# A mixture-of-experts layer: adding the expert outputs to the residual by selection matmuls instead of through DRAM

## Chip, cores, metric

One core of one Trainium2 chip. The metric is the device time of one launch in microseconds; the kernel before took 1423.31 us (median of 3 runs, 1421.72 to 1424.41).

## What is computed

One encoder layer on 512 tokens of width 1024 in f32: four parallel token mixers and their merge, attention over 256 memory tokens, and a mixture of experts; then a last RMSNorm. The mixture sends each token to 2 of 32 experts:

```
h = rmsnorm(x);  group = argmax(h @ w_group + b_group);  two experts = top 2 of softmax(router logits of the group)
for each expert e, on its tokens:  y = (silu(h @ w1[e]) * (h @ w3[e])) @ w2[e]      # 1024 -> 512 -> 1024
x = x + sum over the token's two experts of weight * y;   out = rmsnorm(x) * final_norm
```

## The kernel before

The mixers and the attention fill the first 828 us and are not touched. The mixture has two stages.

**Routing** (L1500 to L1690). The rows after the norm go to DRAM (`xn_scratch`). DVE finds each token's experts and its two weights (`wsel`). `pos` is the token's place in each expert's list, `cnt` an expert's number of tokens. From them come `idx` (the first 64 tokens of each expert, one column an expert) and `idy` (the rows of `ys_scratch` to which the outputs go); a full list of tokens for each expert is written to DRAM by eight scatters of 128 elements (L1855). DVE also makes a table of jobs: one row of four integers for each further block of 64 tokens of an expert that has over 64. With these inputs there is one such overflow job.

**Experts** (from L1695). `experts(lo, hi)` runs on each engine over the 32 experts q, with the job between expert 15 and 16 (`MID` = 16).
- SP loads the weights: six pieces of 1 MB an expert, in order, into a ring of 18 buffers (three experts deep, `DEEP`). A piece is issued when TensorE has used up the one that lies in its buffer (`consumed`, L1744). The job's six pieces take a turn of the ring (L1811), and expert 18 waits for the end of the job (`o_xo`).
- POOL gathers 64 rows an expert from `xn_scratch` (`fetch`, L1839, two experts ahead) and scatters the output to `ys_scratch` (`store`, L1846). For the job it waits for the stores, loads the job's place (a register) and the list, waits for DVE's indices, and gathers (L1867 to L1875).
- PE turns the rows (`turn_rows`, e_x, L1754), multiplies by w1 and w3 (`up`, e_u, L1769: two column halves of 64 tokens side by side), turns the hidden rows (`turn_hidden`, e_h, L1760) and multiplies by w2 (`down`, e_y, L1779). Its order in turn q is up(q), turn_rows(q+1), turn_hidden(q-1), down(q-1).
- ACT copies the turned rows (L1969, L1974), makes tanh and a copy (L1979, L1981), and copies the output to `yo` (L1986). DVE has two products an expert (L2048, L2053).
- At the end SP loads the 4 MB of `ys_scratch` (L1825), DVE adds them to the residual `x_sb`, tile t by tile (L2086, 128 tokens each), and the last norm follows: Square and Sqrt on ACT (L2020, L2022), scaling on DVE (L2080), the store (L1828).

All waits are written out by hand; each engine takes its instructions in the order of the text.

## Time and profile before

| | us |
|---|---|
| median of 3 runs | 1423.31 |
| the profiled execution | 1424.24 |
| its span, first to last instruction | 1422.6 |
| experts, from the first gather to the last scaling | 871.65 to 1419.55 |
| mean granted TensorE clock | 0.963 |

The page gives busy times of the engines, then 40 slices of 35.6 us each: the slices from the 25th on are the experts. A row of the chain says what the end of the program was waiting for at that time; a row of a stretch says how much each engine and the 16 DMA engines were busy in it.

### The profile page before, as it was taken

What the parts mean: (1) busy time and instruction counts of PE and PEld (TensorE: products, weight loads), DVE (VectorE), ACT (ScalarE), POOL (GpSimd) and SP (SyncE); (2) the same over time, 40 slices, a digit from 0 to 9 for tenths busy, and PEclk for the clock granted to TensorE, in tenths of its full rate; (3) what the DMA queues carried; (4) which work ended last, traced back from release to release, by engine and by line L of the source; (5) the groups of instructions that cost most, each with busy time, mean ns of one, the idle gap of its engine ahead of it and who ended that gap; (6) DMA issues with size and microseconds to landing.
All of it is one profiled execution on the core that took longest, in us unless ns stands there. A gap on an engine that the chain in (4) does not pass through costs nothing. (4 is left out here: it accounts for less than half of the span.)

```text
span 1422.6 us, 15467 instructions
## 1 busy us (share of the span) xinstructions
PE 1223.8 (86%) x6254; PEld 828.3 (58%) x6254; DVE 527.9 (37%) x948; ACT 387.3 (27%) x638; POOL 92.2 (6%) x118
## 2 busy tenths in 40 slices
PE   6999999999999988999998864997777489887782
PEld 5887997897687766888886532333333133333330
DVE  4333444667857387445365434110100001010004
ACT  6222232235443432243253220121111112111112
POOL 1000000000000000000000003111111101111100
PEclk9999999999999999999999986999999789999996
DMA  7322213112123212323331069999999979999994
GB/s 266 112 88 76 75 60 115 64 60 82 45 71 107 89 67 100 137 90 107 115 113 66 0 270 322 366 409 408 416 417 407 419 310 396 406 416 415 411 401 184
DMA packets 50470, 301.54 MB, mean 212 GB/s; under 512 B 8882, under 2 KB 9282, under 8 KB 20320
## 3 DMA queue, kind: packets, MB, share of 16 engines
q1 hardware_dynamic: 41792, 281.06, 51.1%
q0 software_dynamic: 8080, 17.41, 3.7%
q10 hardware_dynamic: 528, 2.10, 0.4%
q8 instruction: 50, 0.82, 0.2%
q14 instruction: 20, 0.16, 0.0%
HBM read 296.50 MB, written 12.93 MB: 218 GB/s over the span
## 5 line engine op out<-in xcount | busy, mean ns | idle before, releaser
L1769 PE MATMUL e_u<-w_raw,xT 128*64 128x512 f32 x1056 | 244.0, 608 | 62.1 <-DMA w_raw<-in_w 58.7
L1769 PEld LDWEIGHTS e_u<-w_raw,xT 128*64 128x64 f32 x1056 | 81.6, 139 | 219.7 <-issue 215.6
L2048 DVE SCALAR_TENSOR_TENSOR tn<-tn,e_u 64x512 f32<-64x512 f32 x32 | 21.7, 679 | 429.5 <-ACT tn L1979 429.5
L286 DVE TENSOR_TENSOR s_lo<-s_raw,s_hi 128x2048 fp32r<-128x2048 f32 (+1 forms) x68 | 138.5, 2037 | 42.5 <-ACT s_hi L281 41.5
L281 ACT CAST s_hi<-s_raw 128x2048 fp32r<-128x2048 f32 (+1 forms) x68 | 115.8, 1703 | 104.6 <-PE pz L529 34.7
L1779 PE MATMUL e_y<-w_raw,hidT 128*64 128x512 f32 x528 | 121.9, 604 | 15.4 <-ACT hidT L1974 15.0
L513 PE MATMUL pz<-hT_hi,s_hi 128*128 128x512 f32 x256 | 103.7, 405 | 10.1 <-DVE s_lo L286 10.1
L497 PE MATMUL pz<-hT_hi,s_hi 128*128 128x512 f32 x256 | 102.9, 402 | 0.0
L1969 ACT COPY xT<-e_x 128x512 f32<-128x512 f32 x32 | 18.7, 585 | 306.5 <-PE e_x L1754 306.5
L513 PE MATMUL pz<-hT_hi,s_lo 128*128 128x512 f32 x256 | 101.0, 394 | 0.0
L513 PE MATMUL pz<-hT_lo,s_hi 128*128 128x512 f32 x256 | 100.9, 394 | 0.0
L497 PE MATMUL pz<-hT_lo,s_hi 128*128 128x512 f32 x256 | 99.9, 390 | 0.0
L497 PE MATMUL pz<-hT_hi,s_lo 128*128 128x512 f32 x256 | 99.8, 390 | 0.0
L1779 PEld LDWEIGHTS e_y<-w_raw,hidT 128*64 128x64 f32 x528 | 35.3, 138 | 77.6 <-issue 57.5
L490 PE MATMUL pz<-s_hi,hT_hi 128*128 128x256 f32 x256 | 73.5, 287 | 0.0
L490 PE MATMUL pz<-s_lo,hT_hi 128*128 128x256 f32 x256 | 72.4, 283 | 0.0
L490 PE MATMUL pz<-s_hi,hT_lo 128*128 128x256 f32 x256 | 72.4, 283 | 0.0
L529 PE MATMUL pz<-zR,s_hi 128*128 128x512 f32 x192 | 63.0, 389 | 0.0
L513 PEld LDWEIGHTS pz<-hT_hi,s_hi 128*128 128x128 f32 x256 | 48.7, 190 | 22.6 <-DVE s_lo L286 11.8
L1846 POOL DMA_INDIRECT ys_scratch<-yo,idy x32 | 32.0, 1001 | 390.9 <-ACT yo L1986 390.9
L920 ACT ACTIVATE tg<-pz 128x512 f32<-128x512 f32 x32 | 19.1, 598 | 134.5 <-PE pz L513 134.5
L513 PEld LDWEIGHTS pz<-hT_hi,s_lo 128*128 128x128 f32 x256 | 49.0, 191 | 10.8 <-issue 1.0
(355 smaller groups left out, 1904.9 us busy)
## 6 DMA issues: line engine op xcount, KB each, us to landing
w_raw<-in_w SPq DMA_DIRECT2D x198, 1024.0 KB, 27.3
s_raw<-in_w_mix SPq DMA_DIRECT2D x30, 1024.0 KB, 4.8
s_raw<-in_w_gb SPq DMA_DIRECT2D x32, 768.0 KB, 4.2
s_raw<-in_w_out_pieces SPq DMA_DIRECT2D x4, 1024.0 KB, 5.0
w_raw<-ys_scratch SPq DMA_DIRECT2D x8, 512.0 KB, 6.6
x_sb<-in_x SPq DMA_DIRECT2D x4, 512.0 KB, 4.7
rel_bias<-in_rel_tiles POOLq DMA_DIRECT2D x8, 256.0 KB, 3.1
decay<-in_decay POOLq DMA_DIRECT2D x8, 256.0 KB, 4.0
```

The lines of the kernel that those rows point to most:

```text
L281: nc.scalar.copy(w_hi[n % 2][:, 0:w], w_raw[n % 2][:, 0:w]).then_inc(w_himade, 1)
L286: nc.vector.tensor_tensor(w_lo[n % 2][:, 0:w], w_raw[n % 2][:, 0:w], w_hi[n % 2][:, 0:w].bitcast(F32), ALU.subtract).then_inc(w_split, 1)
L490: last = nc.tensor.matmul(pz[j][:, half * CW:(half + 1) * CW], hp[:, k, at:at + P], wp, start=(k == 0 and m == 0), stop=(k == KD - 1 and m ...
L497: last = nc.tensor.matmul(pz[j][:], wp, hp, start=(k == 0 and m == 0), stop=(k == KD - 1 and m == 2))
L513: last = nc.tensor.matmul(pz[0][:], wp, hp, start=(k == 0 and m == 0), stop=(k == KD - 1 and m == 2))
L529: last = nc.tensor.matmul(pz[1][:], wp, yp[:, k, :], start=(k == 0 and m == 0), stop=(k == KB - 1 and m == 2))
L920: nc.scalar.activation(tg[u % 2][:], pz[0][:], ACT.Tanh, scale=0.5).then_inc(g_tanh, 1)
L1769: m = nc.tensor.matmul(ps_u[o][lo:lo + FIRST, :], xT[b][:, k * FIRST:(k + 1) * FIRST], raw[j][:, kk * FF:(kk + 1) * FF], start=k == 0, sto ...
L1779: m = nc.tensor.matmul(ps_y[o][lo:lo + FIRST, :], hT[b][:, k * FIRST:(k + 1) * FIRST], raw[j][:, kk * D + h * FF:kk * D + (h + 1) * FF], s ...
L1846: pool.indirect_dma_start(ys_halves, bass.IndirectOffsetOnAxis(idy[:, q:q + 1], 0), yo[b][:], None, bounds_check=last_y, oob_is_err=False) ...
L1969: nc.scalar.copy(xT[q % 2][:], ps_x[:]).then_inc(s_xT, 1)
L2048: nc.vector.scalar_tensor_tensor(tn[:], tn[:], 1.0, ps_u[b][0:FIRST, :], ALU.add, ALU.mult).then_inc(s_hm, 1)
```

## The change

- No `ys_scratch`, no `store`, no load of 4 MB at the end, no `idy`. ACT's copy of an output gets the type float32r (`y_hi`), DVE makes the rest `y_lo` = output - `y_hi`.
- After the routing DVE makes `wq` (a token's weight for each expert) and `pos_if` (place + 1 where the token is the expert's), PE turns the latter to `pos_rows` (32 x 512).
- For each expert `select` (one matmul) spreads the expert's row of `pos_rows` over 128 partitions in the PSUM of e_x, and DVE compares it with the slot number (`selected`): `st` is 1 where slot and token meet. `unit(q, t)` multiplies `st` by `y_hi` and `y_lo` for token tile t: 4 matmuls of 64 rows, 128 columns by 512, for the two halves h of the width in the two row halves of the array and two PSUM banks. DVE adds `wq` times the result to `x_sb` (`add`, two instructions a unit). A unit waits for the adds of the one before. The units of expert q-2 stand in turn q: after each half of up, after turn_hidden, and after down(q-1); those of expert 30 stand before down(31), those of 31 at the end.
- The job's list, table row and token rows are fetched by POOL in turns 8 and 10, and DVE makes its indices and weights (`job_ids`) in turn 10. Each job fetches the next one's; there is one fetch more than jobs. The job's outputs are added by 8 matmuls and 8 adds.
- For that the job table, now 17 rows, is written by SP to DRAM a second time with each row 128 times (`job_of_all`), ahead of the loads for expert 3.

The diff, cut:

```diff
...
-        ys_dram = nc.dram_tensor("ys_scratch", [SLOTS, D], F32).ap()
         list_dram = nc.dram_tensor("list_scratch", [EXPERTS * LIST, 1], I32).ap()
         jobs_dram = nc.dram_tensor("jobs_scratch", [1, P], I32).ap()
+        job_of_all = nc.dram_tensor("jobs_wide", [JOBS + 1, P, 4], I32).ap()
...
+                wide = [P, T, EXPERTS]
+                do.after(nc.vector.tensor_tensor(junk[:, 0, :, :], hot[:, 0, :, :],
+                                                 wsel[:, 0, :].unsqueeze(2).to_broadcast(wide), ALU.mult))
+                do.after(nc.vector.tensor_tensor(junk[:, 1, :, :], hot[:, 1, :, :],
+                                                 wsel[:, 1, :].unsqueeze(2).to_broadcast(wide), ALU.mult))
+                do.after(nc.vector.tensor_tensor(wq[:], junk[:, 0, :, :], junk[:, 1, :, :], ALU.add))
...
-                do.after(nc.vector.tensor_scalar(idy[:], idf[:], 2.0, half_no, ALU.mult, ALU.add))
...
+                sp.dma_start(jobs_dram[0:1, 0:4 * (JOBS + 1)].rearrange("o (j q) -> (o j) q", q=4),
+                             jobsi[0:JOBS + 1, :]).then_inc(s_jobs_out, 16)
+                sp.dma_start(job_of_all, jobsi[0:JOBS + 1, :].unsqueeze(1).to_broadcast([JOBS + 1, P, 4])
+                             ).then_inc(s_jobs_wide, 16)
...
+                consumed(sp, END, W2A)
                 sp.dma_start(final_gain, bass.AP(a["rows"].tensor, 0, [[0, P], [1, D]])).then_inc(f_gain, 16)
-                for b in range(2):
-                    sp.wait_ge(s_ys[b], 16 * (EXPERTS // 2))
-                for t in range(T):
-                    for ch in range(2):
-                        r = ch * N + t * P
-                        sp.dma_start(y_of(t, ch), ys_dram[r:r + P, :]).then_inc(f_ld[ch][t], 16)
...
-                def store(q):
-                    b = q % 2
-                    pool.wait_ge(s_yo, q + 1)
-                    pool.indirect_dma_start(ys_halves, bass.IndirectOffsetOnAxis(idy[:, q:q + 1], 0),
-                                            yo[b][:], None,
-                                            bounds_check=last_y, oob_is_err=False).then_inc(s_ys[b], 16)
...
+                def list_of(r):
+                    j = pool.value_load(jobs_dram[0:1, bass.ds(r * 4, 1)], min_val=0,
+                                        max_val=(EXPERTS * LIST - FIRST) // LIST_UNIT)
+                    for lo in (0, FIRST):
+                        pool.dma_start(ibl[lo:lo + FIRST, :], list_dram[bass.ds(j * LIST_UNIT, FIRST), :].bitcast(U32)
+                                       ).then_inc(s_lst, 16)
+                    pool.dma_start(jb[:], job_of_all[bass.ds(r, 1), :, :].rearrange("o p q -> (o p) q")
+                                   ).then_inc(s_lst, 16)
+
+                def rows_of_job():
+                    pool.indirect_dma_start(xo[:], None, xn_dram,
+                                            bass.IndirectOffsetOnAxis(ibx[0:FIRST, :], 0),
+                                            bounds_check=last_x, oob_is_err=False).then_inc(o_xs, 16)
+
                 for q in range(MID):
                     fetch(q + 2)
-                    if q:
-                        store(q - 1)
-                store(MID - 1)
-                pool.wait_ge(s_scattered, 16 * 2 * T)
-                pool.wait_ge(s_jobs_out, 16)
+                    if q == LIST_AT:
+                        pool.wait_ge(s_scattered, 16 * 2 * T)
+                        pool.wait_ge(s_jobs_out, 16)
+                        pool.wait_ge(s_jobs_wide, 16)
+                        list_of(0)
+                    if q == LIST_AT + 2:
+                        pool.wait_ge(s_ids, 1)
+                        pool.wait_ge(o_zero, 1)
+                        rows_of_job()
...
+                        pool.wait_ge(o_cu, r * 8 + 8)
                         pool.sem_inc(s_turn, 1)
-                        pool.indirect_dma_start(xo[:], None, xn_dram,
-                                                bass.IndirectOffsetOnAxis(ibx[0:FIRST, :], 0),
-                                                bounds_check=last_x, oob_is_err=False).then_inc(o_xs, 16)
-                        pool.wait_ge(o_yo, r + 1)
+                        list_of(r + 1)
+                        pool.wait_ge(s_ids, r + 2)
                         pool.sem_inc(s_turn, 1)
-                        pool.indirect_dma_start(ys_halves, bass.IndirectOffsetOnAxis(iby[:], 0),
-                                                yoo[:], None,
-                                                bounds_check=last_y, oob_is_err=False).then_inc(o_ys, 16)
-                        pool.wait_ge(o_ys, r * 16 + 16)
+                        rows_of_job()
...
-                for q in range(MID, EXPERTS):
-                    if q + 2 < EXPERTS:
-                        fetch(q + 2)
-                    if q > MID:
-                        store(q - 1)
-                store(LAST)
-                for b in range(2):
-                    pool.wait_ge(s_ys[b], 16 * (EXPERTS // 2))
+                pool.wait_ge(o_xs, n * 16 + 16)
+                pool.sem_inc(s_turn, 1)
+                for q in range(MID, EXPERTS - 2):
+                    fetch(q + 2)
...
+                    wait(pe, c_S, q - 2 + (q == MID))
...
+                        combine(q, half)
...
+                def select(q):
+                    pe.wait_ge(s_xT, MID if q + 2 == MID else min(q + 3, EXPERTS))
+                    if q == 0:
+                        pe.wait_ge(c_rows, 1)
+                    nc.tensor.matmul(ps_x[:], one_of[:, q:q + 1].to_broadcast([EXPERTS, P]), pos_rows[:],
+                                     start=True, stop=True).then_inc(c_sel, 1)
+
+                def unit(q, t):
+                    if t == 0:
+                        pe.wait_ge(c_S, q + 1)
+                        pe.wait_ge(s_yo, q + 1)
+                        pe.wait_ge(s_ylo, q + 1)
+                    wait(pe, c_a, 8 * q + 2 * t)
+                    for i, y in enumerate((y_hi, y_lo)):
+                        for h in range(2):
+                            lo = h * FIRST
+                            ins = nc.tensor.matmul(ps_c[h][:], st[lo:lo + FIRST, t * P:(t + 1) * P],
+                                                   y[q % 2][lo:lo + FIRST, :], start=i == 0, stop=i == 1)
+                            if i:
+                                ins.then_inc(c_u, 1)
+
+                def combine(q, t):
+                    if q >= 2:
+                        unit(q - 2, t)
...
+                        combine(q, 2)
+                        if q > lo:
                             down(q - 1)
+                        combine(q, 3)
+                        if q:
+                            select(q - 1)
+                    if hi == EXPERTS:
+                        for t in range(T):
+                            combine(hi, t)
+                        select(hi - 1)
                     turn_hidden(hi - 1)
                     down(hi - 1)

                 pe.sem_inc(o_xo, 1)
+                pe.wait_ge(c_pos, 1)
+                for t in range(T):
+                    last = nc.tensor.transpose(ps_c[0][0:EXPERTS, t * P:(t + 1) * P], pos_if[:, t, :], ident[:])
+                last.then_inc(c_prow, 1)
...
-                            m = down_half(half, 0, 0, OVER + n_)
-                        m.then_inc(o_dn, 1)
-                        pe.wait_ge(o_yo, r + 1)
+                            y = down_half(half, 0, 0, OVER + n_)
+                        y.then_inc(o_dn, 1)
+                        pe.wait_ge(o_m, r * 4 + 4)
+                        pe.sem_inc(s_turn, 1)
+                        for t in range(T):
+                            last = nc.tensor.transpose(ps_c[0][0:FIRST, t * P:(t + 1) * P], m_job[:, t, :], ident[:])
+                        last.then_inc(o_st, 1)
+                        pe.wait_ge(o_S, r + 1)
+                        pe.wait_ge(o_yo, r * 2 + 2)
                         pe.sem_inc(o_xo, 1)
+                        for u in range(2 * T):
+                            t, h = divmod(u, 2)
+                            if u >= 2:
+                                pe.wait_ge(o_ca, r * 8 + u - 1)
+                            nc.tensor.matmul(ps_c[u % 2][:], st_job[:, t * P:(t + 1) * P], y_job[:, h, :],
+                                             start=True, stop=True).then_inc(o_cu, 1)
+                        pe.wait_ge(o_ca, r * 8 + 8)
+                        pe.sem_inc(s_turn, 1)
                     pe.nop()
                 experts(MID, EXPERTS)
+                for t in range(T):
+                    combine(EXPERTS + 1, t)
...
-                    wait(act, s_ys[q % 2], 16 * (q // 2))
-                    nc.scalar.copy(yo[q % 2][:], ps_y[q % 2][:]).then_inc(s_yo, 1)
+                    wait(act, c_u, 8 * (q - 1))
+                    nc.scalar.copy(y_hi[q % 2][:], ps_y[q % 2][:]).then_inc(s_yo, 1)
...
-                        nc.scalar.copy(yoo[:], ps_y[0][:]).then_inc(o_yo, 1)
+                        for h in range(2):
+                            nc.scalar.copy(y_job[:, h, :], ps_y[0][h * FIRST:(h + 1) * FIRST, :]).then_inc(o_yo, 1)
+                        act.wait_ge(o_st, r + 1)
+                        nc.scalar.copy(st_job, ps_c[0][0:FIRST, :]).then_inc(o_S, 1)
...
+                def positions():
+                    do.after(nc.vector.tensor_scalar(pos[:], pos[:], 1.0, None, ALU.add))
+                    nc.vector.scalar_tensor_tensor(pos_if[:], wq[:], 0.0, pos[:], ALU.is_gt, ALU.mult
+                                                   ).then_inc(c_pos, 1)
+                    do.after(nc.vector.tensor_scalar(slot1[:], half_no, -float(FIRST), rank1, ALU.mult, ALU.add))
+                    do.after(nc.vector.tensor_copy(one_of[:], ident[0:EXPERTS, 0:EXPERTS]))
+                    dve.wait_ge(c_prow, 1)
+                    nc.vector.tensor_copy(pos_rows[:], ps_c[0][0:EXPERTS, :]).then_inc(c_rows, 1)
+
+                def selected(q):
+                    dve.wait_ge(c_sel, q + 1)
+                    wait(dve, c_u, 8 * q)
+                    nc.vector.tensor_scalar(st[:], ps_x[:], slot1[:], None, ALU.is_equal).then_inc(c_S, 1)
+
+                def y_rest(q):
+                    dve.wait_ge(s_yo, q + 1)
+                    nc.vector.tensor_tensor(y_lo[q % 2][:], ps_y[q % 2][:], y_hi[q % 2][:].bitcast(F32), ALU.subtract
+                                            ).then_inc(s_ylo, 1)
+
+                def add(q, t):
+                    for h in range(2):
+                        dve.wait_ge(c_u, 8 * q + 2 * t + h + 1)
+                        wait(dve, c_a, 8 * (q - 1) + 2 * t + h + 1)
+                        xt = x_sb[:, t, h * FF:(h + 1) * FF]
+                        nc.vector.scalar_tensor_tensor(xt, ps_c[h][:], wq[:, t, q:q + 1], xt, ALU.mult, ALU.add
+                                                       ).then_inc(c_a, 1)
+
+                def combine(q, t):
+                    if q >= 2:
+                        add(q - 2, t)
+
+                positions()
...
+                        if q == LIST_AT + 2:
+                            job_ids(0)
+                        combine(q, 0)
+                        combine(q, 1)
...
+                        combine(q, 2)
+                        if q > lo:
+                            y_rest(q - 1)
+                        combine(q, 3)
+                        if q:
+                            selected(q - 1)
+                    if hi == EXPERTS:
+                        for t in range(T):
+                            combine(hi, t)
+                        selected(hi - 1)
+                    y_rest(hi - 1)
...
+                    dve.wait_ge(s_lst, r * 48 + 48)
+                    after(nc.vector.tensor_scalar(ib2[:], ibl[:], float(N), -float(N), ALU.is_ge, ALU.mult))
+                    nc.vector.tensor_tensor(ibx[:], ibl[:], ib2[:], ALU.add).then_inc(s_ids, 1)
+                    after(nc.vector.tensor_copy(jf[:], jb[:]))
+                    after(nc.vector.tensor_scalar(jf[:, 2:3], jf[:, 1:2], -float(LIST), 1.0, ALU.mult, ALU.add))
+                    after(nc.vector.scalar_tensor_tensor(jf[:, 2:3], jf[:, 0:1], float(LIST_UNIT), jf[:, 2:3],
+                                                         ALU.mult, ALU.add))
...
+                    for t in range(T):
+                        nc.vector.tensor_scalar(m_job[:, t, :], slot_no[:, 0:FIRST], posj[:, t:t + 1], wj[:, t:t + 1],
+                                                ALU.is_equal, ALU.mult).then_inc(o_m, 1)
...
+                        for u in range(2 * T):
+                            t, h = divmod(u, 2)
+                            xt = x_sb[:, t, h * FF:(h + 1) * FF]
+                            dve.wait_ge(o_cu, r * 8 + u + 1)
+                            nc.vector.tensor_tensor(xt, ps_c[u % 2][:], xt, ALU.add).then_inc(o_ca, 1)
+                        job_ids(r + 1)
...
-                    for ch in range(2):
-                        dve.wait_ge(f_ld[ch][t], 16)
-                        ins = nc.vector.scalar_tensor_tensor(x_sb[:, t, :], y_of(t, ch), wsel[:, ch, t:t + 1],
-                                                             x_sb[:, t, :], ALU.mult, ALU.add)
-                        if ch == 0:
-                            do.after(ins)
-                    ins.then_inc(f_x, 1)
+                    combine(EXPERTS + 1, t)
...
```

## Rows read from the trace of the kernel before

**Rows 1.** The page: busy times, DMA in 40 slices.
```profile
PE 1223.8 (86%) x6254; PEld 828.3 (58%) x6254; DVE 527.9 (37%) x948; ACT 387.3 (27%) x638; POOL 92.2 (6%) x118
DMA  7322213112123212323331069999999979999994
```

**Rows 2.** The chain of waits through two rounds of the ring: start, us, what.
```profile
1258.25 29.44 DMA w_raw<-in_w
1287.82 3.65 PE e_u L1769 x16
...
1293.45 3.68 PE e_y L1779 x16
...
1301.07 6.80 SPq L1483
1307.91 27.24 DMA w_raw<-in_w
1335.29 3.65 PE e_u L1769 x16
```

**Rows 3.** Stretches: PE, PEld, DVE, ACT, POOL busy (x count), clock, DMA share, GB/s.
```profile
892.00:896.00 4.00, 4.00 (x22) 1.34 (x20) 1.36 (x2) 0.62 (x2) 0.16 (x1) 1.00 0.64 175
1148.00:1152.00 4.00, 1.53 (x6) 0.85 (x8) 1.36 (x2) 1.38 (x3) 0.00 (x0) 0.81 0.54 229
1152.00:1156.00 4.00, 4.00 (x16) 1.08 (x12) 0.00 (x0) 0.00 (x0) 0.00 (x0) 0.77 0.04 18
1156.00:1160.00 4.00, 2.16 (x16) 1.34 (x16) 0.00 (x0) 1.17 (x2) 1.02 (x1) 1.00 0.55 150
```

**Rows 4.** DMA queues, 1112:1128 (two stores land), 1128:1148 (none), 1180:1370.
```profile
DMA packets 1125, 6.74 MB, mean 421 GB/s; under 512 B 281, under 2 KB 281, under 8 KB 325
...
DMA packets 1238, 8.43 MB, mean 422 GB/s; under 512 B 208, under 2 KB 208, under 8 KB 209
...
q0 software_dynamic: 2000, 3.63, 5.5%
```

**Rows 5.** Timeline of TensorE: one turn under full clock, then a pair of 64-row matmuls, one float32r.
```profile
1180.39 7.04 PE L1769 MATMUL e_u<-w_raw,xT 128*64 128x512 f32 x32
1192.88 1.46 PE L1769 MATMUL e_u<-w_raw,xT 128*64 128x512 f32 x6
...
176.28 1.13 PE L549 MATMUL pa<-zT 64*128 64x512 f32 x4
...
700.69 0.39 PE L768 MATMUL pa<-s_hi,m_lo 128*128 128x512 f32 x1
700.91 0.39 PE L768 MATMUL pa<-s_hi,m_hi 128*128 128x512 f32 x1
```

**Rows 6.** Timeline at the job and in the last turns.
```profile
1129.65 0.98 POOL L1875 DMA_INDIRECT xo<-xn_scratch,ibx  x1 [5.71 <-DVE ibx L2065]
1136.07 1.11 PE L1754 MATMUL e_x<-ident,xo 64*128 64x64 f32 x8 [18.79 <-DMA xo<-xn_scratch,ibx]
1381.74 3.65 PE L1769 MATMUL e_u<-w_raw,xT 128*64 128x512 f32 x16 [1.32 <-DMA w_raw<-in_w]
1386.94 0.68 DVE L2048 SCALAR_TENSOR_TENSOR tn<-tn,e_u 64x512 f32<-64x512 f32 x1 [12.53 <-ACT tn L1979]
1394.91 0.59 ACT L1986 COPY yo<-e_y 128x512 f32<-128x512 f32 x1 [3.75 <-PE e_y L1779]
1404.56 1.06 ACT L2020 ACTIVATE w_raw<-x_sb 128x1024 f32<-128x1024 f32 x1 [9.05 <-DVE x_sb L2086]
1418.27 1.28 DVE L2080 SCALAR_TENSOR_TENSOR x_sb<-x_sb,f_ss,w_raw 128x1024 f32<-128x1024 f32 x1
```

**Rows 7.** The job table's DMA, and DMA packets in 7.55:8.2 (small tables load) and 877:895.
```profile
875.10 0.34 SPq L1791 DMA_DIRECT2D jobs_scratch<-jobsi  x1
...
DMA packets 332, 0.27 MB, mean 422 GB/s; under 512 B 176, under 2 KB 304, under 8 KB 316
...
DMA packets 986, 4.34 MB, mean 241 GB/s; under 512 B 424, under 2 KB 424, under 8 KB 489
```

94 lines of the change are left out of this document (53 added, 41 removed).

## The prediction, made before the changed kernel ran

> **What bounds the kernel now.** I read the page first: TensorE is busy 86% of the span, but in the experts' slices the DMA row stands at 9 almost everywhere, and it drops in one place, about two thirds of the way [rows 1]. Then the chain of waits: two rounds of the ring (three experts each) look the same. A piece of w waits 27 to 29 us in the queue, TensorE uses it, the freed buffer lets SP issue the next one, and SP itself then sits up to 6.8 us in an issue because the queue is full. Three experts take 1335.29 - 1287.82 = 47.5 us, 15.8 us a turn [rows 2]. TensorE alone needs 1192.88 - 1180.39 = 12.5 us for a turn when it is behind and never waits [rows 5]. So from about 900 us to 1387 us the weight stream sets the end: 33 turns (32 experts and the job), and TensorE has 3.3 us of slack in each. Three things lie outside that rule: the DMA hole at the job, 1149 to 1158 [rows 3]; the tail from the last landing on [rows 6]; and the start, where small DRAM writes hold the stream back [rows 7]. The change touches all three, and the stream as well.
>
> **The stores go.** 31 of the 33 stores run beside the stream (those of experts 30 and 31 don't). In 1112:1128, where two stores and no gather land, the queues moved 6.74 MB, of which 6.54 MB on the hardware queue; in 1128:1148, with neither, that queue moved 8.43 MB in 20 us, 0.4215 MB/us [rows 4]. 6.54 MB would take 15.5 us of the 16, so a store costs 0.24 us. In 1180:1370 POOL's queue has 5.5% of 190 us, 10.5 us for 13 stores and 12 gathers, 0.42 us each [rows 4]. The weights alone are 6.29 MB a turn, 14.9 us at that rate, so store and gather together cost 15.8 - 14.9 = 0.9 us, and a store at most some 0.6. I take 0.35, near the two direct rows: 31 x 0.35 = 11 us less (7.5 to 19).
>
> **The job comes early.** PE idles 18.8 us before the job's first matmul at 1136.07, waiting for a gather that POOL issued at 1129.65 [rows 6]. Its DMAs and indices move to turns 8 and 10, on POOL and DVE, which are mostly idle (POOL 92 us of the span, DVE 528 [rows 1]). The gain is not the 18.8 us of PE but the hole in the stream that they cause, since expert 18 waits for the job: (0.46 + 0.96 + 0.45) x 4 = 7.5 us [rows 3]. I take 7 (5 to 7.5). What is late next is the job's own weights, which were issued from 1099.83 on and land while PE would now start; PE is then some 20 us ahead of where it was. The job's 8 new matmuls and adds come after `o_xo` is given, so they don't hold the loads. The fetch after the last job (list, table row, DVE's indices, rows) holds POOL and the first adds of turn 16 some 15 us; the gathers for 16 and 17 are already issued, and that of 18 is wanted a turn later. Cost nothing; if that cover fails, 2 to 4 us of PE's slack.
>
> **What TensorE and DVE get.** A unit is 4 matmuls of 512 columns. A pair of f32 matmuls on the two row halves, 4 records, took 1.13 us [rows 5]: one after the other, 8 passes at full clock would be 1.7, so the halves run side by side. A float32r matmul of 512 columns follows the last by 0.22 us [rows 5], so a unit is 2 x 0.22, with its weight loads 0.5 us; four are 2.0, `select` 0.3, and one unit falls into the wait for hidT that PE has anyway (0.4): some 1.9 us a turn, 14.4 in all. The stream will need 15.8 - 0.35 = 15.45. DVE gets 8 adds, `selected` and `y_rest`, each like the 512-column product of 0.68 us [rows 6]: 6.8 + 1.4 = 8.2 us a turn. The waits between them fit: two adds (1.4) lie beside each half of up (3.5), the third pair beside down. So in the stream this costs nothing (bound: 3.1 us a turn before it does). ACT does the same copies.
>
> **The tail.** Before: from up's second half at 1381.74 to the end of the last scaling at 1419.55, 37.8 us [rows 6]. After, from the same landing: half of up 3.4, unit 0.5, turn_hidden and its copy 1.2, unit 0.5 (it waits 0.5 for the adds), down(30) 3.4: 1391.2. The copy, `y_rest`, two adds and `selected` are 0.3 + 0.6 + 0.7 + 1.4 + 0.7 = 3.7: 1394.9. Only then may the units of expert 30 start, and each waits for the adds of the one before, 0.8 + 1.4 = 2.2 us: four take 8.8, 1403.7. down(31) is queued on PE behind the last of them (1402.1): `select` 0.3, turn 0.5, copy 0.7, down 3.7, output copy 0.7, `y_rest` 0.7, first unit 0.7: 1409.4. Its adds 1.4, Square 1.3; then three tiles at adds 1.4 + scaling 1.5 + 0.2 = 3.1, and the last scaling 1.9: 1423.3. So what goes (store, load, 10.4 us of adds) is less than what comes, and the tail grows by 3.7 us (-1, if units run ahead of the adds, to +7).
>
> **The start.** `idy` leaves the way to `idx`: 0.3 us less. The weights `wq` and `positions` lie in waits of DVE and beside the first gather.
>
> Sum so far: -11 - 7 + 3.7 - 0.3 = -14.6 us.
>
> **The wide table.** SP now writes 17 x 128 pieces of 16 bytes, 2176, to DRAM on the queue that carries the weights, behind the small table (875.10 [rows 7]) and ahead of expert 3. No row shows such a write, so I bound it. Two questions: on how many engines, and how long a piece. All transfers of this trace have 16, 64 or 128 rows and fall in equal shares on the 16 DMA engines. 17 rows can't: the only equal share is all on one. I take one engine, and the weights queue behind it there, since each piece of w needs all 16. Time of a piece: at the low end, where small tables load, 332 packets passed in 0.65 us, 16 x 0.65 / 332 = 31 ns each on an engine, and their bytes alone (422 GB/s) explain that, so less than 31, even next to nothing, is possible. At the high end are the eight scatters into DRAM: in 877:895 the queues moved 4.34 MB where 18 us at 0.4215 would be 7.6, a loss of 7.7 us for 7 x 8 = 56 elements an engine, 137 ns each [rows 7]. I take 31, the nearer in kind (hardware queue, one packet a piece; but a load): 2176 x 0.031 = 68 us (0 to 298). Nothing covers it: the stream has been the bound since 900, and the hole in 892:896 (0.36 x 4 = 1.4 us) is the scatters' doing [rows 3].
>
> The Trainium skill bears on the first question: "DMA: Bandwidth & Descriptors", section "Why a DMA increments its semaphore by 16 and not by 1", says that a DMA uses the largest number of engines up to 16 that divides the slowest dimension of both sides, which for 17 is one. Its section "Bandwidth" has about 10.5 ns for a small packet, an estimate of 23 us for 2176; no row here shows either. By these the sum would be about 1432.
>
> **Forecast.** 1424.2 - 14.6 + 68 = 1477.6 for a profiled execution; the median of the runs is 0.9 lower: 1476.7 us.
>
> **Rivals.**
> - The table is spread over 16 engines, 136 pieces each: 4 us at 31 ns (19 at 137). Then 1423.3 - 14.6 + 4 = 1412.7, faster. For it: the small table's DMA has always been cheap, 128 copies could be shared out. Against: the outer count is 17.
> - One engine, but under 17 ns a piece: 0 to 36 us, about 1430. For it: the low bound above.
> - One engine at the scatters' price: 298 us, 1707. Against: those are single elements at scattered places from another queue.
> - TensorE becomes the bound, slower too: if the pairs of a unit don't overlap (16 x 0.22 = 3.6) and the waits for adds show (0.5 and select 0.3), a turn is 12.5 + 4.4 = 16.9 us, over the 15.45 by 1.4, in about 25 turns 35 us; it decides above 3.1 us a turn. With a table of 4 us: 1448. Against: the 1.13 us pair.
>
> **Chances.** Forecast (one engine, 17 to 81 ns) 0.36; spread 0.34 (0.30 faster, 0.03 same, 0.01 slower); cheap on one engine 0.10; very dear 0.08; TensorE 0.12 (0.10 slower, 0.02 same). That is 0.30 faster, 0.05 within 0.2% (what a measurement can tell from no change), 0.65 slower. The likeliest case alone spans 1445 to 1585. With the spread case's low end the range is 1404 to 1585; outside lie the dear case and little else.
>
> **What would show it.** The landing of `jobs_wide`: some 70 us after 890 in the forecast, under 20 if spread; in the first, the DMA row falls to almost nothing between 900 and 970 and PE waits for w in turn 3. The turn of the ring should be 15.4 to 15.5 us with PE idle for about 1 us in it; a turn of 16 or more with no waits for w means TensorE. The DMA row should have no hole at the job, and PE should wait there for the job's weights. In the tail, the adds of expert 30 should stand ahead of down(31), and from the last landing to the last scaling it should be 41 to 42 us.

## The result, and the profile after

The changed kernel took 1468.92 us (median of 4 runs, 1465.53 to 1470.7), the kernel before on the same chip 1423.86: the ratio is 1.031 (95% interval 1.0291 to 1.033). The change costs 45 us. The number of the forecast, 1476.7, was near. Its sum was not: a term that was too large stood in for one that was missing, as the experiments show.

The page after, first its busy times and slices (to be read beside [rows 1]; a slice is 36.7 us now), then the chain by engine and the line of the adds:

```profile
PE 1344.1 (92%) x6822; PEld 875.0 (60%) x6822; DVE 749.1 (51%) x1302; ACT 388.2 (26%) x640; POOL 62.9 (4%) x90
...
DMA  7222132221123114223220395999999969999931
...
PE 24%; DMA 7%; SPq 4%; DVE 3%; issue 2%; ACT 1%; POOLq 0%; POOL 0%; DVEq 0%; ACTq 0%
...
L2134 DVE SCALAR_TENSOR_TENSOR x_sb<-e_c,wq,x_sb 128x512 f32<-128x512 f32 x256 | 179.7, 742 | 162.4 <-PE e_c L1946 162.4
```

The chain by engine of the kernel before:

```profile
DMA 18%; PE 13%; SPq 5%; DVE 1%; ACT 1%; issue 1%; POOLq 0%; POOL 0%; ACTq 0%
```

TensorE's busy time rose by 120 us. The DMA row now has a 5 at the 25th slice and a 6 at the 33rd, where the row of before has a 9 and a 7. In the chain DMA stood first; now TensorE does, with DMA far behind.

Where the time went, by stretches of turns. A turn begins with TensorE's first matmul of up (e_u in its timeline). Turns 0 to 15 are experts 0 to 15, turn 16 is the job, and turns 17 to 32 are experts 16 to 31. Differences within the profiled execution are compared, since turn 0 starts anywhere between 880 and 886 us:

| us | turn 1 to 6 | 6 to 15 | 15 to 22 (job) | 22 to 32 | 32 to last scaling |
|---|---|---|---|---|---|
| before | 62.7 | 144.3 | 119.7 | 158.5 | 42.8 |
| after | 85.4 | 140.1 | 142.3 | 154.0 | 50.9 |
| difference | +22.7 | -4.2 | +22.6 | -4.5 | +8.2 |

So there are three losses, at the start, the job and the tail, and small gains in the two long stretches between.

**The start.** Stretches of the kernel after, where the wide table is written:

```profile
896.00:904.00 8.00, 7.53 (x42) 3.34 (x40) 1.36 (x2) 1.93 (x4) 0.94 (x1) 1.00 0.44 76
904.00:916.00 12.00, 12.00 (x63) 4.71 (x59) 4.04 (x6) 1.03 (x2) 0.21 (x1) 1.00 0.12 6
916.00:924.00 8.00, 5.41 (x25) 1.84 (x25) 5.48 (x9) 2.06 (x5) 0.72 (x1) 1.00 0.55 33
924.00:928.00 4.00, 0.00 (x0) 0.00 (x0) 0.00 (x0) 0.00 (x0) 0.00 (x0) 0.50 0.86 346
```

and the DMA packets of its stretch 904:916:

```profile
DMA packets 1066, 0.08 MB, mean 6 GB/s; under 512 B 1051, under 2 KB 1051, under 8 KB 1066
```

For over 12 us the queues move 6 GB/s, nearly all of it in packets under 512 bytes. The packet records have the 16-byte pieces from 897.2 to 922.3 us: 2193 of them, 17 being the small table's, mostly about 85 in a microsecond. Then TensorE, which had loads for three experts, has nothing to do (924:928).

**The job.** Timeline of TensorE, kernel after:

```profile
1141.49 1.07 PE L1769 MATMUL e_x<-ident,xo 64*128 64x64 f32 x8 [1.70 <-DVE y_lo L2126]
1143.23 10.06 PE L1784 MATMUL e_u<-w_raw,xT 128*64 128x512 f32 x32 [0.68 <-ACT xT L2070]
...
1163.77 11.85 PE L2018 MATMUL e_c<-xo,st_job 64*128 64x512 f32 x16 [1.52 <-ACT st_job L2080]
1176.87 1.11 PE L1769 MATMUL e_x<-ident,xs 64*128 64x64 f32 x8 [1.25 <-DVE x_sb L2213]
...
1190.58 0.50 PE L1946 MATMUL e_c<-y_hi,st 64*128 64x512 f32 x2 [1.69 <-DVE x_sb L2134]
```

and stretches of it, with the clock in the third column from the end:

```profile
1163.00:1176.00 13.00, 11.85 (x16) 4.05 (x16) 5.19 (x8) 0.53 (x1) 0.00 (x0) 0.63 1.01 427
...
1201.00:1205.00 4.00, 4.00 (x22) 1.29 (x20) 1.41 (x2) 0.00 (x0) 0.00 (x0) 1.00 0.00 0
1205.00:1209.00 4.00, 4.00 (x26) 2.25 (x22) 1.22 (x2) 0.39 (x1) 0.15 (x1) 1.00 0.00 0
```

The job's rows are there early (its first matmul waits 1.70 us, and for `y_lo`, not for a gather), and the hole of [rows 3] is gone from 1149. But eight f32 matmuls take 11.85 us. The granted clock changes between its two levels, 1.2 and 2.4 GHz, in that stretch; 0.63 is its mean. And the hole has moved: at 1201 to 1209 the DMA share is 0.00. SP issues nothing from 1189.3 to 1211.9 us; the buffer that it wants next holds weights of expert 16, whose down TensorE begins only at 1209.91. TensorE is busy in those rows, and DMA is not. That is the reverse of what [rows 2] showed.

**The long stretches.** TensorE's timeline of one turn, kernel after, beside [rows 5]:

```profile
1234.23 3.65 PE L1784 MATMUL e_u<-w_raw,xT 128*64 128x512 f32 x16
1237.81 0.50 PE L1946 MATMUL e_c<-y_hi,st 64*128 64x512 f32 x2
1238.15 0.40 PE L1946 MATMUL e_c<-y_lo,st 64*128 64x512 f32 x2
1238.39 0.99 PE L1769 MATMUL e_x<-ident,xs 64*128 64x64 f32 x8
1239.22 0.64 PE L1775 MATMUL e_h<-ident,hd 64*128 64x64 f32 x4
1240.05 0.50 PE L1946 MATMUL e_c<-y_hi,st 64*128 64x512 f32 x2 [0.18 <-DVE x_sb L2134]
1240.38 0.40 PE L1946 MATMUL e_c<-y_lo,st 64*128 64x512 f32 x2
1240.71 3.65 PE L1794 MATMUL e_y<-w_raw,hidT 128*64 128x512 f32 x16
1244.29 0.50 PE L1946 MATMUL e_c<-y_hi,st 64*128 64x512 f32 x2
...
1244.96 0.50 PE L1934 MATMUL e_x<-pos_rows,one_of 32*128 32x512 f32 x1
1245.38 3.65 PE L1784 MATMUL e_u<-w_raw,xT 128*64 128x512 f32 x16
```

From 1234.23 to the same place of the next turn, 1249.63, it is 15.40 us, and TensorE waits for no weights in it: the only wait that its rows show is the 0.18 us for an add. The predicted turn was 15.45, but as the stream's, with TensorE idle for about 1 us.

**The tail.** TensorE's timeline, kernel after:

```profile
1432.56 0.80 PE L1946 MATMUL e_c<-y_hi,st 64*128 64x512 f32 x2 [2.29 <-DVE st L2122]
...
1435.28 0.79 PE L1946 MATMUL e_c<-y_hi,st 64*128 64x512 f32 x2 [1.50 <-DVE x_sb L2134]
...
1443.80 6.53 PE L1794 MATMUL e_y<-w_raw,hidT 128*64 128x512 f32 x16 [0.46 <-ACT hidT L2037]
1451.95 0.50 PE L1946 MATMUL e_c<-y_hi,st 64*128 64x512 f32 x2 [1.62 <-DVE y_lo L2126]
```

and a stretch of it:

```profile
1435.00:1440.00 5.00, 2.44 (x8) 1.01 (x8) 2.38 (x5) 0.00 (x0) 0.00 (x0) 0.50 0.00 0
```

The structure is the predicted one, units of expert 30 ahead of down(31). The units are 2.72 us apart, not 2.2, at the lower level of the clock (0.50), and down(31) takes 6.53 us where it took 3.65 in the turns.

### The profile page after: what moved, and what is told of

The parts are those of the page before. It is cut to its first block and busy times, and to the rows that moved or that the text cites. A ratio compares the mean times of both kernels' runs of the same rounds, so it can differ in the third digit from the quotient of the medians.

```text
span 1468.8 us, 17299 instructions
## 1 busy us (share of the span) xinstructions
PE 1344.1 (92%) x6822; PEld 875.0 (60%) x6822; DVE 749.1 (51%) x1302; ACT 388.2 (26%) x640; POOL 62.9 (4%) x90
## 5 line engine op out<-in xcount | busy, mean ns | idle before, releaser
L1784 PE MATMUL e_u<-w_raw,xT 128*64 128x512 f32 x1056 | 251.0, 620 | 13.6 <-DMA w_raw<-in_w 10.7
L2134 DVE SCALAR_TENSOR_TENSOR x_sb<-e_c,wq,x_sb 128x512 f32<-128x512 f32 x256 | 179.7, 742 | 162.4 <-PE e_c L1946 162.4
L1784 PEld LDWEIGHTS e_u<-w_raw,xT 128*64 128x64 f32 x1056 | 74.0, 141 | 154.5 <-issue 151.1
L1794 PE MATMUL e_y<-w_raw,hidT 128*64 128x512 f32 x528 | 124.9, 616 | 1.9 <-ACT hidT L2037 1.4
L513 PE MATMUL pz<-hT_hi,s_hi 128*128 128x512 f32 x256 | 103.7, 405 | 10.1 <-DVE s_lo L286 10.1
L1946 PE MATMUL e_c<-y_hi,st 64*128 64x512 f32 x256 | 66.3, 515 | 25.2 <-DVE x_sb L2134 21.3
L1946 PEld LDWEIGHTS e_c<-y_hi,st 64*128 64x128 f32 x256 | 24.7, 189 | 107.4 <-DVE x_sb L2134 53.4
L490 PE MATMUL pz<-s_lo,hT_hi 128*128 128x256 f32 x256 | 72.4, 283 | 0.0
L490 PE MATMUL pz<-s_hi,hT_lo 128*128 128x256 f32 x256 | 72.4, 283 | 0.0
L1300 DVE SCALAR_TENSOR_TENSOR tg<-tg,pz 128x512 f32<-128x512 f32 x24 | 16.5, 687 | 96.3 <-PE pz L529 96.3
L513 PEld LDWEIGHTS pz<-hT_hi,s_hi 128*128 128x128 f32 x256 | 48.8, 191 | 22.6 <-DVE s_lo L286 11.8
```

The costliest lines, as they stand in the source:

```text
L490: last = nc.tensor.matmul(pz[j][:, half * CW:(half + 1) * CW], hp[:, k, at:at + P], wp, start=(k == 0 and m == 0), stop=(k == KD - 1 and m ...
L513: last = nc.tensor.matmul(pz[0][:], wp, hp, start=(k == 0 and m == 0), stop=(k == KD - 1 and m == 2))
L1784: m = nc.tensor.matmul(ps_u[o][lo:lo + FIRST, :], xT[b][:, k * FIRST:(k + 1) * FIRST], raw[j][:, kk * FF:(kk + 1) * FF], start=k == 0, sto ...
L1794: m = nc.tensor.matmul(ps_y[o][lo:lo + FIRST, :], hT[b][:, k * FIRST:(k + 1) * FIRST], raw[j][:, kk * D + h * FF:kk * D + (h + 1) * FF], s ...
L1946: ins = nc.tensor.matmul(ps_c[h][:], st[lo:lo + FIRST, t * P:(t + 1) * P], y[q % 2][lo:lo + FIRST, :], start=i == 0, stop=i == 1)
L2134: nc.vector.scalar_tensor_tensor(xt, ps_c[h][:], wq[:, t, q:q + 1], xt, ALU.mult, ALU.add).then_inc(c_a, 1)
```

## Experiments

Ratios are to the kernel before, measured beside each. Stretches of all kernels that the text uses; they are of one profiled execution each, the median is of all runs:

| us | 1 to 6 | 6 to 15 | 15 to 22 | 22 to 32 | 32 to end | median | ratio (interval) |
|---|---|---|---|---|---|---|---|
| after without the wide table | 74.7 | 138.6 | 140.3 | 154.0 | 50.9 | 1456.55 | 1.0221 (1.0191 to 1.0251) |
| before + table, 17 rows | 87.3 | 142.7 | 117.3 | 158.3 | 42.8 | 1451.72 | 1.0198 (1.0165 to 1.0231) |
| before + table, 16 rows | 72.4 | 143.4 | 117.4 | 158.7 | 42.8 | 1434.51 | 1.0077 (1.0047 to 1.0107) |
| no table, no next job | 74.7 | 138.6 | 136.0 | 154.0 | 49.5 | 1452.76 | 1.0199 (1.0168 to 1.0229) |
| no table, no y_lo | 71.0 | 131.3 | 140.0 | 144.7 | 47.7 | 1429.01 | 1.0024 (1.0005 to 1.0044) |
| no table, other tail | 74.7 | 138.6 | 139.5 | 154.0 | 44.5 | 1451.14 | 1.0186 (1.0155 to 1.0218) |
| before, job early | 63.1 | 143.6 | 113.2 | 159.7 | 42.7 | 1420.55 | 0.9972 (0.9957 to 0.9988) |
| before, no stores | 62.5 | 136.4 | 112.9 | 153.2 | 42.9 | 1406.01 | 0.9869 (0.9837 to 0.9900) |
| before, more on TensorE | 78.8 | 141.7 | 144.2 | 157.4 | 44.4 | 1471.42 | 1.0328 (1.031 to 1.0347) |
| three mendings | 74.7 | 138.6 | 143.2 | 154.0 | 44.5 | 1450.84 | 1.018 (1.0153 to 1.0206) |
| job early, rows of 4 KB | 62.5 | 142.6 | 114.6 | 159.8 | 44.6 | 1421.71 | 0.9981 (0.9971 to 0.9991) |
| mendings and one pass | 71.0 | 130.2 | 128.6 | 144.7 | 42.0 | 1415.50 | 0.9925 (0.9905 to 0.9944) |

### The wide table: out of the changed kernel, and into the kernel before

```diff
-                sp.dma_start(job_of_all, jobsi[0:JOBS + 1, :].unsqueeze(1).to_broadcast([JOBS + 1, P, 4])
-                             ).then_inc(s_jobs_wide, 16)
...
-                    pool.dma_start(jb[:], job_of_all[bass.ds(r, 1), :, :].rearrange("o p q -> (o p) q")
+                    pool.dma_start(jb[:], jobs_dram[0:1, bass.ds(r * 4, 4)].to_broadcast([P, 4])
```

> The changed kernel without the table job_of_all: POOL loads the job's row of four integers straight from jobs_scratch, repeated over 128 partitions; everything else stays. Theory A (the wide table holds the weight stream once and the delay is never won back, because TensorE's turn of 15.4 us is as long as the stream's): the first piece of expert 3 lands near 902 instead of 932.7 us, PE no longer idles in turn 3, and the time falls by the 24 us of lag seen at turn 6: about 1445 us (1438 to 1448). Rival B (the table's delay would have been swallowed later anyway, since TensorE is the bound over the whole stretch): it falls by less than 12 us, 1457 us or more, and turns 4 to 15 become longer than 15.5 us. If even this comes out below 1424, the table was the whole loss.

The two others add to the kernel before, with 17 and with 16 rows:

```diff
+                sp.dma_start(job_of_all, jobsi[0:17, :].unsqueeze(1).to_broadcast([17, P, 4])
+                             ).then_inc(s_jobs_wide, 16)
```

> The kernel before with the wide write of 17 x 128 pieces of 16 bytes added behind the small job table, and nothing else (nobody reads it). Theory A (one DMA engine writes all 2176 pieces, 11.5 us a thousand, and the weights wait for it): 1424 + 25 to 30 = 1449 to 1454 us less what the stream can win back before the end (its turn of 15.8 us is the bound there, so nothing). Theory C (the delay comes from SP, which can't issue while its queue is full, not from the writing): also slow, but with packets of the table done early and weights of expert 3 issued late. Theory B (the write is cheap and the loss in the changed kernel has another origin): within 5 us of before.

> The same as the run with 17 rows, but 16 rows: 2048 pieces of 16 bytes. Theory A (17 rows can only go to one engine, 16 rows go to all 16): 128 pieces an engine at 12 ns are 1.5 us, at most 4: 1425 to 1429 us. Rival (the number of small pieces is what costs, on however many engines): 16/17 of the cost of the run with 17 rows, 1447 to 1452 us.

Measured: without the table 1456.55, only 12.4 us less. In the kernel before, the same table costs 27.5 us (1451.72 against 1424.20; the interval is 23.5 to 32.9, as the runs lie between 1443.78 and 1454.04). The profiled execution is the fastest of them; it loses 24.6 us between turns 1 and 6 (87.3 against 62.7) and wins some 4 back later. With 16 rows the table costs 10.3 us, between the 1 to 5 of theory A and the 23 to 28 of its rival. Stretches of before + 17 rows, then of before + 16 rows:

```profile
900.00:904.00 4.00, 4.00 (x20) 1.29 (x18) 1.36 (x2) 1.31 (x3) 0.00 (x0) 1.00 0.12 1
...
916.00:920.00 4.00, 0.00 (x0) 0.00 (x0) 0.00 (x0) 0.51 (x1) 1.96 (x2) 1.00 0.35 33
```

```profile
896.00:900.00 4.00, 4.00 (x22) 1.48 (x19) 0.00 (x0) 0.00 (x0) 0.00 (x0) 1.00 1.66 205
900.00:904.00 4.00, 3.53 (x22) 1.86 (x23) 1.36 (x2) 1.92 (x4) 0.00 (x0) 1.00 0.84 43
904.00:908.00 4.00, 4.00 (x20) 1.29 (x18) 0.00 (x0) 0.58 (x1) 1.58 (x2) 1.00 0.96 47
```

17 rows trickle at a DMA share of 0.12; with 16 rows nearly all pieces start within 3 us (of 2064 16-byte packets 1779 between 897 and 900), and the rest of the time passes in few, slow packets. One row more makes the table take 29 us (894.1 to 923.2) in place of 10 (897.1 to 907.6). This is what the forecast's account, one engine against 16, would make, but the records don't name engines, so it is not shown directly. A share of 0.12 and not a sixteenth fits one engine only if its packet records overlap, as those of 16 rows do (1.66 at 896:900). Theory C of that run is out: SP does stand from 885.6 to 920.9 us, but the table's packets are not done early.

What the run without the table added is more important than its 12.4 us: its turns 2 to 6 are 15.40 us each, with all loads there, where the kernel before took 12.5. Neither theory of that run holds alone. The first got right that TensorE no longer waits for the weights of expert 3, but not the 24 us; the second got the size of what comes back nearly right, but turns 4 to 15 did not become longer than 15.5 us (138.6 us from turn 6 to 15).

### TensorE's own turn

```diff
-                    for i, y in enumerate((y_hi, y_lo)):
+                    for i, y in enumerate((y_hi,)):
```

> As the run without the wide table (1456.6 us), and each unit makes only the two matmuls of y_hi; those of y_lo are left out, so the outputs lose the rest y_lo. All waits and DVE's adds stay. Theory A (TensorE is the bound over nearly the whole stage: its turn of 12.5 + 4 x 0.67 + 0.43 - nothing hidden = 15.4 leaves no room to catch up, where the kernel before catches up at 12.5): a unit falls by 0.33 us, so a turn behind the stream takes 14.1 us; turn 6 starts 4 to 5 us earlier than in that run and the total falls by the part of 31 x 1.33 = 41 us that the stream allows, 20 to 30 us: 1427 to 1437. Rival B (DVE's adds and the waits for them set the turn): the turns stay at 15.4 and the total falls by less than 5 us.

In the kernel before, nothing but work for TensorE is added:

```diff
+                        if half:
+                            for cols in (512, 512, 512, 192):
+                                nc.tensor.matmul(ps_c[:, 0:cols], xT[q % 2][:, 0:P], xT[q % 2][:, 0:cols],
+                                                 start=True, stop=True)
```

> The kernel before with nothing but more work on TensorE: in every expert's turn, between the halves of up, three matmuls of f32 of 512 columns (0.87 us each) and one of 192 columns, into a bank that nobody reads; 2.9 us a turn, which brings TensorE's own turn to 15.4 us as in the changed kernel. Stores, table, job and tail are those of before. Theory A (the mean turn of 15.8 us hides that TensorE runs at 12.5 us in turns 2 to 5 and after the job, to eat up loads that are already there; with 15.4 us that is 4 x 2.9 = 11.6 us later each time, and only some 0.5 us a turn is won back at the stream's pace): turn 6 starts 11 to 12 us later, and the end comes 10 to 20 us later, 1434 to 1444 us. Rival B (the prediction's step: 15.4 is under 15.8, so it costs nothing): within 3 us of 1424.

Measured: one pair of matmuls less a unit, 27.5 us less (1429.01 against 1456.55), the turn 14.46 instead of 15.40 (144.7 us from turn 22 to 32 are ten such turns). The pair is worth 0.93 / 4 = 0.23 us, not 0.33; DVE's adds and their waits are all still there, and TensorE waits 0.19 us a turn for them. The other way round, 3.24 us more a turn (15.74, as the pieces of 512 columns took more than planned) cost the kernel before 47.3 us, with its stores, its table and its tail as they were. Some 5 us of that are turn 0 (15.0 against 10.1). Timeline of TensorE in it:

```profile
948.07 3.60 PE L1770 MATMUL e_u<-w_raw,xT 128*64 128x512 f32 x16
951.61 3.17 PE L1910 MATMUL e_c<-xT 128*128 128x512 f32 x8
...
963.82 0.60 PE L1770 MATMUL e_u<-w_raw,xT 128*64 128x512 f32 x2
```

I had expected 10 to 20 us. Theory A was right in kind and too small: I had let the stream win time back, but at 15.74 us TensorE is no faster than the stream of 15.8, so every wait, the one at the job above all (turns 15 to 22: 144.2 against 119.7), stays in the time to the end.

This is the missing term. Two stretches of the kernel before, turns 2 to 5 and those behind the job:

```profile
904.00:954.00 50.00, 48.12 (x242) 19.04 (x238) 5.45 (x8) 10.04 (x20) 7.83 (x8) 1.00 1.01 407
1167.00:1218.00 51.00, 48.45 (x242) 19.12 (x241) 6.81 (x10) 11.11 (x22) 6.80 (x7) 1.00 1.02 389
```

TensorE is busy 48.1 of 50 and 48.5 of 51 us. It is the bound there: it works off three experts' loads that lie ready, at 12.5 us a turn, and so wins back what it had waited for. The slack of 3.3 us a turn, read from the steady rounds, was not free; it was spent in eight turns.

### The job

```diff
-                        list_of(r + 1)
...
+                        with pool.If(n > r + 1):
+                            list_of(r + 1)
...
-                        job_ids(r + 1)
+                        with dve.If(n > r + 1):
+                            job_ids(r + 1)
```

> As the first run (no wide table), and the fetch of a next job with its index work on DVE is made only if there is a next job; with one job it falls away. Theory A (that fetch holds DVE until 1189 us, with it the adds of turn 16 on which TensorE's units wait, and so the buffers of experts 16 and 17 come free late: the hole of about 13 us in the loads at 1197 to 1213): against the first run 10 to 14 us less, near 1432 us, and no stretch of zero DMA share behind the job. Rival (the loss at the job is TensorE's own work there, at half clock: 10.1 us of up, 11.9 us of eight matmuls of f32): less than 5 us of gain, 1440 or more.

> The kernel before with one part of the change alone: list and rows of the first job are fetched in turns 8 and 10, its indices made on DVE in turn 10, and a next job's only where there is one; the outputs still go through DRAM with the stores. Theory A (the hole in the loads at 1149 to 1158 us is worth its 7.5 us, and the stream has no other limit there): 5 to 7.5 us less than before, 1417 to 1419 us, with no stretch of low DMA share at the job. Rival (experts 16 to 18 find their buffers full or the stream catches up in any case): within 2 us of 1424.

The second is the kernel before with only the list and the rows fetched in turns 8 and 10 (and a next job's only where there is one); its main edit:

```diff
+                    if q == MID // 2:
+                        pool.wait_ge(s_scattered, 16 * 2 * T)
+                        pool.wait_ge(s_jobs_out, 16)
+                        list_of(0)
+                    if q == MID // 2 + 2:
+                        pool.wait_ge(s_ids, 2)
+                        pool.wait_ge(o_zero, 1)
+                        rows_of_job()
```

Measured: without the fetch of a job that doesn't exist the kernel takes 3.8 us less (1452.76 against 1456.55), so the rival of that run holds. Not all of it need be the fetch's. Of the 4.3 us by which turns 15 to 22 differ in the two traces, 3.3 lie in turn 16 (30.96 against 34.21), ahead of the fetch, where down of the job took 3.65 against 5.35 us and the eight matmuls 11.74 against 13.33, at different clocks. Behind it, turns 17 and 18 together differ by 1.0 (35.17 against 36.14). Timeline of TensorE without that fetch: eight matmuls still take 11.74 us.

```profile
1148.33 11.74 PE L2015 MATMUL e_c<-xo,st_job 64*128 64x512 f32 x16 [1.52 <-ACT st_job L2077]
1161.35 1.11 PE L1768 MATMUL e_x<-ident,xs 64*128 64x64 f32 x8 [1.28 <-DVE x_sb L2210]
```

A hole stays in the loads too, as a stretch of the same kernel shows (DMA share 0.10):

```profile
1188.00:1196.00 8.00, 7.81 (x46) 3.75 (x44) 4.32 (x8) 1.93 (x4) 0.93 (x1) 1.00 0.10 27
```

The early fetch in the kernel before gains 3.5 us (the interval of the ratio is 1.7 to 6.1 us), less than the 5 to 7.5 of theory A and more than the 2 of its rival. In its trace turns 15 to 22 are 6.5 us shorter, turns 22 to 32 are 1.2 us longer, and the stream has no hole:

```profile
1148.00:1156.00 8.00, 7.33 (x40) 2.89 (x38) 1.36 (x2) 1.65 (x3) 1.92 (x2) 1.00 1.02 378
```

This part of the change is worth having by itself: it makes a kernel 0.3% faster than before.

### The stores

```diff
-                    if q:
-                        store(q - 1)
...
-                        sp.dma_start(y_of(t, ch), ys_dram[r:r + P, :]).then_inc(f_ld[ch][t], 16)
+                        sp.dma_start(y_of(t, ch), xn_dram[r % N:r % N + P, :]).then_inc(f_ld[ch][t], 16)
```

> The kernel before without the stores of the outputs of experts 0 to 29 (30 stores; those of 30, 31 and the job stay); in place of ys_scratch the end loads xn_scratch, as many bytes, so the outputs are not the layer's. The prediction's term (a store costs the stream 0.35 us, bounds 0.24 to 0.6): 30 x 0.35 = 10.5 us less, 1413.7 (1406 to 1417), turns of the ring of 15.45 us. Rival (the stores' packets fill gaps of the queue that the weights leave): within 3 us of 1424.

> The kernel before with the job fetched early, and the output of an expert stored as 64 rows of 4 KB instead of 128 half rows of 2 KB (two copies of ACT of 64 x 512 in place of one of 128 x 512). The run without stores put 0.6 us on a store. Theory P (a store costs by its rows or descriptors): half of that goes, 33 x 0.3 = 10 us less than the 1420.6 of the run with the early job alone, 1410 to 1413. Theory Q (a store costs by its bytes, or by what the slowest engine still has to do): within 2 us of 1420.

Measured: without the 30 stores it is 18.0 us less, 0.60 each. But the run changes the job too: POOL has no stores to wait for, issues the gather of the job's rows at 1106.99 and not at 1129.65, and TensorE waits 3.12 us for them and not 18.79:

```profile
1114.10 1.11 PE L1754 MATMUL e_x<-ident,xo 64*128 64x64 f32 x8 [3.12 <-DMA xo<-xn_scratch,ibx]
```

Its stream has no hole at the job either. So the early job is part of the 18.0, alone worth 3.5 us. Away from the job, turns 1 to 15 are 8.1 us shorter (0.58 a turn) and turns 22 to 32 are 5.3 us shorter (0.53 a turn): a store costs the stream 0.5 to 0.6 us, still near the upper bound of the forecast. What the stream can do without stores is 15.3 us a turn (153.2 / 10 from turn 22 to 32); the first stretch begins with a turn at TensorE's 12.5 us and is no measure of it. Stores of whole rows changed nothing (1421.71 and 1420.55, overlapping), but their page has the same 8080 packets on POOL's queue, so the run says nothing on the price of a packet. The pages of the kernels before and without the 30 stores:

```profile
q0 software_dynamic: 8080, 17.41, 3.7%
...
HBM read 296.50 MB, written 12.93 MB: 218 GB/s over the span
```

```profile
q0 software_dynamic: 5680, 13.41, 3.0%
...
HBM read 296.50 MB, written 5.07 MB: 215 GB/s over the span
```

The queue has 4.0 MB and 2400 packets less, 0.133 MB and 80 packets a store, about the rows in use. The count of bytes written to HBM is 7.86 MB less, 0.262 MB a store, which is all 128 half rows that the instruction names, used or not; the packets don't bear it out as traffic. At 0.4215 MB/us [rows 4] the first makes 0.32 us and the second 0.62 us. A store's 0.5 to 0.6 us is more than the bytes of the queue explain; no run varied the number of rows in use, so whether the unused rows cost is open.

### The tail, and the mendings together

```diff
+                    turn_hidden(hi - 1)
+                    down(hi - 1)
                     if hi == EXPERTS:
                         for t in range(T):
                             combine(hi, t)
                         select(hi - 1)
-                    turn_hidden(hi - 1)
-                    down(hi - 1)
```

> As the run without the wide table (1456.6 us), but turn_hidden(31) and down(31) stand before the units of expert 30, and y_rest(31) between their adds. Theory A (in the tail the units of 30, 2.7 us apart because each waits for adds, stand in front of down(31), and TensorE's clock falls in those waits): the end comes 7 to 10 us earlier, 1447 to 1450, with down(31) at 3.7 us instead of 6.5. Rival (the chain of adds of 30 and 31 on DVE sets the end whatever the order on TensorE, 16 adds of 0.74 us): under 3 us.

> The changed kernel with three mendings together, its outputs still those of the layer: no wide table, no fetch for a job that doesn't exist, down(31) ahead of the units of 30. If they add up (-12.4, -3.8 and -5.4 us seen one by one): 1468.9 - 21.6 = 1447 us (1445 to 1449), still slower than before, because TensorE's turn of 15.4 us stays. If the conditional fetch only moved a wait, nearer 1451.

Measured: the other order gains 5.4 us (1451.14), and the end comes 44.5 us after turn 32 instead of 50.9. The tail is 6.4 us shorter and down(31) is back at 3.65 us, with TensorE's clock at its upper level (1.00 in 1414:1418). Adds and units by turns are then the chain, so less came than the 7 to 10 expected. With the conditional fetch as well it is 1450.84: the 3.8 us of that did not add. The traces show why one execution can hide it. Turns 17 and 18, behind the fetch, are 3.5 us shorter than with the other tail alone (35.05 against 38.54), but turn 16, ahead of it, is 7.1 us longer (38.15 against 31.03): the job's up took 9.74 us and not 7.09, its down 6.57 and not 3.65, and the eight matmuls 13.33 and not 11.84, at a clock that was at the lower level for more of the time, as in the first microseconds of up:

```profile
1127.67 9.74 PE L1783 MATMUL e_u<-w_raw,xT 128*64 128x512 f32 x32 [0.68 <-ACT xT L2067]
```

```profile
1127.67:1132.50 4.83, 4.83 (x12) 1.48 (x14) 0.00 (x0) 0.00 (x0) 0.00 (x0) 0.50 1.01 427
```

TensorE's work up to there is the same in the two kernels. So at the job, differences of a few us between single traces can be the clock's and not the edit's. How the clock fell in the runs without a profile is not on record in such detail, and why the medians don't add stays open.

The last kernel takes TensorE's passes away as well: only y_hi in the units, and the job's eight matmuls in one pass (`st_job` and the job's outputs as float32r).

> All mendings of the changed kernel together (no wide table, next job fetched only where there is one, down(31) ahead of the units of 30), and one pass of float32r in place of exact products: the units make only the matmuls of y_hi, and the job's eight matmuls take outputs and weighted selection rounded to float32r, one pass instead of four. The outputs are rounded to float32r by that before they are added. Theory A (TensorE is the bound, so each of its passes counts): from the 1429.0 us of the run without y_lo, 5 for the tail and 7 to 9 for the job's matmuls (11.7 us before, at half clock): 1415 to 1418 us, below the kernel before. Rival (at the job and in the tail the waits between DVE and TensorE stay as they are, and the matmuls hide in them): 1421 to 1425 us.

Measured: 1415.50, ratio 0.9925 (0.9905 to 0.9944), the fastest kernel here that computes the layer, though with outputs rounded to float32r. Turns 15 to 22 took 128.6 us, where those of the kernels with exact products took 136.0 to 143.2; the eight matmuls of the job run from 1138.73 to 1144.52, 5.8 us with their waits, where they took 11.7 to 13.3. The time lies in the 1415 to 1418 of theory A. So the idea of the change can pay, by 0.7% here: it needs TensorE's share cut, not DMA's.

## Why the prediction was right, and where it was not

- **The forecast case.** Its direction was right, and 1468.92 lies in its range. Its condition was not met: it asked for a piece of 17 ns or more. What came is the condition of the rival "one engine, but under 17 ns a piece", which had a chance of 0.10 and a time of about 1430. The time fell into the forecast's range only because TensorE cost what the table did not.
- **The signs.** The stall came in kind: TensorE waits 8.78 us for the weights of expert 3, with a DMA share of 0.12 ahead of it. But the table's last piece starts at 922.3 us, some 30 us after 890 and not some 70.
- **The term of 68 us** was mis-sized: a piece took 11.5 ns (25 us for 2176), not 31. The low bound's reasoning, that 31 ns was explained by bytes, spoke for this. In the kernel before the table costs 27.5 us, in the changed one 12.4; TensorE would have been 12 us late there anyway (74.7 us from turn 1 to 6 without the table, against 62.7). The Trainium skill's "DMA: Bandwidth & Descriptors" has about 10.5 ns for a packet in its section "Bandwidth"; the trace's 11.5 ns comes near it. Its section "Why a DMA increments its semaphore by 16 and not by 1" has one engine for 17 rows; the runs with 17 and 16 rows fit that, though no record names an engine.
- **"In the stream this costs nothing"** is the step that failed. Without the table the sum would have said 1409, and the kernel took 1456.6. Two parts: the turn was to be 14.4 and is 15.40. The pairs do run side by side (0.23 us each), but the units lengthen the turn by 0.81, 0.63, 0.39 and 0.76 us in their four places, 2.6 us where the sum had 1.6 (2.0 less 0.4 in the wait for hidT), and `select` by 0.43 and not 0.3. The 0.4 was right: down has no wait for hidT left (0.47 before), and there a unit costs only 0.39. So each unit is some 0.3 us longer than its pairs, an estimate from these rows; the sum had next to nothing for that. And the bound of 3.1 us was compared with a mean turn, while TensorE needed its speed in the turns behind each wait. The rival "TensorE becomes the bound" was the second mechanism at work, with its condition (3.1 us) too high.
- **The stores**, -11: at 0.5 to 0.6 us each, 31 of them cost the stream 16 to 19, but that gain was not collected in full, since TensorE's 15.40 us and not the stream's 15.3 sets the turn, with no turns of 12.5 left. Only some 4 us came in each long stretch (15.85 to 15.40 a turn in the second).
- **The job**, -7: 3.5 alone (6.5 in the trace), in the direction and nearly of the size. "Come after `o_xo`, so they don't hold the loads" failed: the eight matmuls, 11.85 us at a reduced clock, hold TensorE, and through its next turns the buffers. The next job's fetch, "cost nothing", cost 3.8 by the medians and 1.0 to 3.5 by the turns behind it, about its own fallback of 2 to 4.
- **The tail**, +3.7: +8.2 from the start of turn 32, one over the bound. Each unit is 0.5 us longer (2.72) and down(31) 2.9, both at the lower clock, which the sum took at full speed.
- So -14.6 should have been about +32, and 68 about 12. That the two errors cancel is luck, and so is the place in the likeliest case's range. The sign is what the reasoning earned: with the table's 27.5 us in place of 68 the sum would have given some 1436, slower still.

## What to carry to other kernels

An engine with slack in the mean turn may be spending it: look for stretches where it runs without a wait behind each stall, and add up what a stall costs if it can't run faster than the stream afterwards. A DMA of many tiny pieces does not belong on the queue that feeds the bound, and its outer count matters: 17 rows cost the kernel before 27.5 us, 16 rows 10.3. Repeat a row while reading, not while writing, as the run without the table does. Where a gain was expected from a transfer, check first that the transfer's engine would still be the bound after the change.
